# Low parts of the weight tiles on VectorE, rounding of h on ScalarE, in a two-layer streaming encoder

## The reference, cut to what matters

```python
D_MODEL, SEQ, DEPTH = 1024, 512, 2          # D_FF = 2816
for l in range(DEPTH):
    ada = (silu(c) @ w_ada[l] + b_ada[l]).reshape(B, 9, D_MODEL)
    u = modulate(rmsnorm(x, norm_g[l, 0]), ada[:, 0], ada[:, 1])
    x = x + 0.5 * ada[:, 2] * swiglu(u, w_ff1_up[l], w_ff1_down[l])
    u = modulate(rmsnorm(x, norm_g[l, 1]), ada[:, 3], ada[:, 4])
    x = x + ada[:, 5] * token_mixing(u, ...)      # window attention + causal pools, two gates, w_out
    u = modulate(rmsnorm(x, norm_g[l, 2]), ada[:, 6], ada[:, 7])
    x = x + 0.5 * ada[:, 8] * swiglu(u, w_ff2_up[l], w_ff2_down[l])
# swiglu(u): a, b = split(u @ w_up); (silu(a) * b) @ w_down
# token_mixing: z = u @ w_in; q, k, v, p, g_a, g_p = split(z)
#   merged = sigmoid(g_a) * (attention(q, k, v) @ w_attn_o) + sigmoid(g_p) * (pools(p) @ w_pool_o)
#   merged @ w_out
```

## Time and profile before

| what | value |
|---|---|
| median of 3 runs | 2163.26 us (2158.65 to 2165.34) |
| span of the profiled execution | 2167.4 us |
| TensorE busy | 2103.8 us |
| VectorE busy | 987.4 us |
| GpSimd busy | 955.2 us |
| ScalarE busy | 571.0 us |
| mean granted TensorE clock | 0.978 |

### The profile page before, as it was taken

The page is one execution under the profiler, slowest core; times in us unless marked ns, Lnnn a source line. Parts: engine busy times, 40 slices in busy tenths (PEclk is TensorE's granted clock), DMA queues, the critical chain, the costliest instruction groups (busy, mean ns, idle before and its releaser), DMA issues.

```text
span 2167.4 us, 30219 instructions
## 1 busy us (share of the span) xinstructions
PE 2103.8 (97%) x10214; PEld 1775.1 (82%) x10214; DVE 987.4 (46%) x1609; ACT 571.0 (26%) x850; POOL 955.2 (44%) x471
## 2 busy tenths in 40 slices
PE   7999999998999999999999999999989999999999
PEld 7888888886887888878888888888868788888887
DVE  5733234268658643223345422335856766332332
ACT  1322222231422422222222222222233224123222
POOL 0644344345245554334445533444443456443443
PEclk6999999999999999999999999999999999999999
DMA  7344345332345355254425524442423544432333
GB/s 272 108 136 140 91 146 163 71 117 83 93 127 183 88 162 161 68 146 137 136 59 172 155 75 145 137 134 67 141 69 112 156 151 126 131 100 79 98 100 104
DMA packets 343634, 267.49 MB, mean 123 GB/s; under 512 B 27094, under 2 KB 306990, under 8 KB 343470
## 3 DMA queue, kind: packets, MB, share of 16 engines
q1 hardware_dynamic: 341792, 264.80, 40.8%
q10 hardware_dynamic: 1678, 0.55, 0.1%
HBM read 263.21 MB, written 2.10 MB: 122 GB/s over the span
## 4 chain that ended last, share of the span: by engine, by line
PE 79%; issue 12%; POOL 5%; DVE 2%; DMA 1%; ACTq 0%; DVEq 0%; POOLq 0%; ACT 0%; SPq 0%
PE bank L1214 23%; PE bank L1215 22%; PE bank L1216 22%; POOL w_lo L561 5%; PE bank L1277 1%; PE bank L1278 1%; PE bank L1281 1%; PE ps L1485 1%; PE ps L1299 1%; POOL pool_s L575 1%; PE ps L1237 1%; PE ps L1236 1%; PE ps L1235 1%; PE bank L1235 1%; PE bank L1237 1%
## 5 line engine op out<-in xcount | busy, mean ns | idle before, releaser
L561 POOL TENSOR_TENSOR w_lo<-stage,w_hi 128x1024 fp32r<-128x1024 f32 (+2 forms) x342 | 856.8, 2519 | 1107.2 <-ACT w_hi L619 1060.2
L1214 PE MATMUL bank<-u_hi,w_hi 128*128 128x512 f32 x1792 | 713.2, 398 | 10.5 <-issue 7.5
L1215 PE MATMUL bank<-u_lo,w_hi 128*128 128x512 f32 x1792 | 701.4, 391 | 0.0
L1216 PE MATMUL bank<-u_hi,w_lo 128*128 128x512 f32 x1792 | 701.3, 391 | 0.0
L619 ACT ACTIVATE w_hi<-stage 128x1024 fp32r<-128x1024 f32 (+2 forms) x340 | 353.5, 1071 | 207.2 <-DMA stage<-in_w_pool_o 66.3
L1214 PEld LDWEIGHTS bank<-u_hi,w_hi 128*128 128x128 f32 x1792 | 339.2, 189 | 82.9 <-issue 11.8
L1216 PEld LDWEIGHTS bank<-u_hi,w_lo 128*128 128x128 f32 x1792 | 338.9, 189 | 72.0
L1215 PEld LDWEIGHTS bank<-u_lo,w_hi 128*128 128x128 f32 x1792 | 339.4, 189 | 70.9 <-issue 2.9
L1214 PE MATMUL bank<-h_hi,w_hi 128*128 128x512 f32 x744 | 292.1, 393 | 6.1 <-POOL w_lo L561 6.1
L909 DVE TENSOR_TENSOR prod<-silu,bank 128x512 f32<-128x512 f32 x88 | 60.5, 687 | 515.9 <-PE bank L1216 493.1
L889 DVE SCALAR_TENSOR_TENSOR ada_acc<-ada_stage,c_act,ada_acc 128x512 f32<-128x512 f32 x252 | 268.0, 1064 | 52.5 <-DMA ada_stage<-in_w_ada 47.9
(11 more groups left out here) (160 smaller groups left out, 1680.6 us busy)
## 6 DMA issues: line engine op xcount, KB each, us to landing
stage<-in_w_ff_up SPq DMA_DIRECT2D x176, 512.0 KB
ada_stage<-in_w_ada SPq DMA_DIRECT2D x256, 256.0 KB, 3.5
stage<-in_w_ff_down SPq DMA_DIRECT2D x32, 1408.0 KB
stage<-in_w_in SPq DMA_DIRECT2D x18, 1024.0 KB
stage<-in_w_out SPq DMA_DIRECT2D x10, 1024.0 KB
ada_first<-in_w_ada SPq DMA_DIRECT2D x16, 512.0 KB, 12.2
stage<-in_w_in SPq DMA_DIRECT2D x16, 256.0 KB
stage<-in_w_in SPq DMA_DIRECT2D x8, 512.0 KB
```

Of the source, the lines that this page charges most:

```text
L561: nc.gpsimd.tensor_tensor(stage_tile(w_lo, kind, n), t, hi_tile(n, depth(kind, n)), ALU.subtract).then_inc(lo_ready, 1)
L1214: mm(bank[n % BANKS][:, :], hi[:, k, :], rhs_hi(k), start=(k == 0), stop=False)
L1215: mm(bank[n % BANKS][:, :], hi[:, k, :], rhs_lo(k), start=False, stop=False)
L1216: last = mm(bank[n % BANKS][:, :], lo[:, k, :], rhs_hi(k), start=False, stop=(k == k_n - 1))
```

## The change

VectorE makes the low parts of the weight tiles in the layers (in the mix at the front of its step for steps 0 to 5 and 26 to 49, and behind the step's other work, ahead of the ada pieces, for steps 6 to 25; in the feed-forward stages at the front of every step). GpSimd keeps the low parts of u, the pools' sums, and the first tiles before the layers. ScalarE rounds the product to h_hi, after it has rounded the weights in the same odd step, and waits for the product for that. In an odd step VectorE does its ada piece between the product and h_lo.

```diff
--- before.py
+++ after.py
@@ -589,12 +589,8 @@
                 low_part("ff", 0, n)
             with pool.Fori(0, DEPTH) as l:
                 u_low(l, 0)
-                with pool.Fori(0, 2) as half:
-                    for n in range(FF_TILES):
-                        low_part("ff", tiles_before(l, 0, half), n + AHEAD)
                 u_low(l, 1)
                 for n in range(MIX_TILES):
-                    low_part("mix", tiles_before(l, 1), n + AHEAD)
                     if n == 1:
                         for t in (*pool_in, *pool_s):
                             nc.gpsimd.memset(t[:, 0:PAD], 0.0).then_inc(pads_zeroed, 1)
@@ -602,9 +598,6 @@
                     if T_P - 1 <= n < T_P + 3:
                         window_sums(l, n - T_P + 1)
                 u_low(l, 2)
-                with pool.Fori(0, 2) as half:
-                    for n in range(FF_TILES):
-                        low_part("ff", tiles_before(l, 2, half), n + AHEAD)
 
 
 
@@ -647,6 +640,10 @@
                             act.wait_ge(product_ready, products_before(l, i, half) + j - 1)
                         nc.scalar.activation(silu[:, j % 2, :], bank[n % BANKS][:, :], ACT.Silu
                                              ).then_inc(silu_ready, 1)
+                    if n < 2 * HALF_FT and n % 2 == 1:
+                        j = n // 2
+                        act.wait_ge(product_ready, products_before(l, i, half) + j + 1)
+                        nc.scalar.activation(h_hi[:, j, :], prod[:, j % 2, :], ACT.Copy).then_inc(h_hi_ready, 1)
                     if n >= 2 * HALF_FT:
                         square(x_before(l, i, half), n - 2 * HALF_FT, adds_before(l, i, half))
 
@@ -772,6 +769,13 @@
                     ins = nc.vector.scalar_tensor_tensor(y, t, 1.5, y, ALU.add, ALU.mult)
                 ins.then_inc(newton, 1)
 
+            def low_part(kind, base, n):
+
+                dve.wait_ge(hi_ready, base + n + 1)
+                t = stage_tile(stage, kind, n)
+                nc.vector.tensor_tensor(stage_tile(w_lo, kind, n), t, hi_tile(n, depth(kind, n)),
+                                        ALU.subtract).then_inc(lo_ready, 1)
+
             def vectors(l, i):
 
                 count = l * VEC_STEPS + 2 + i * 3
@@ -900,6 +904,7 @@
                 tiles = tiles_before(l, i, half)
                 count = products_before(l, i, half)
                 for n in range(FF_TILES):
+                    low_part("ff", tiles, n + AHEAD)
                     if n < 2 * HALF_FT and n % 2 == 1:
                         j = n // 2
                         dve.wait_ge(silu_ready, count + j + 1)
@@ -908,8 +913,8 @@
                             dve.wait_ge(h_lo_ready, count + j)
                         nc.vector.tensor_tensor(prod[:, j % 2, :], silu[:, j % 2, :], bank[n % BANKS][:, :], ALU.mult
                                                 ).then_inc(product_ready, 1)
-                        dve.wait_ge(product_ready, count + j + 1)
-                        nc.vector.tensor_copy(h_hi[:, j, :], prod[:, j % 2, :]).then_inc(h_hi_ready, 1)
+                        if n < FF_ADA:
+                            ada_piece(l, i, half, n)
                         dve.wait_ge(h_hi_ready, count + j + 1)
                         nc.vector.tensor_tensor(h_lo[:, j, :], prod[:, j % 2, :], h_hi[:, j, :], ALU.subtract
                                                 ).then_inc(h_lo_ready, 1)
@@ -919,7 +924,7 @@
                         ada_group(l, i, half, n // 8 - 1)
                     if n == 18:
                         make_gate(l, i, half)
-                    if n < FF_ADA:
+                    if n < FF_ADA and (n % 2 == 0 or n >= 2 * HALF_FT):
                         ada_piece(l, i, half, n)
 
             def read_tile(tiles, n, dst):
@@ -1053,6 +1058,8 @@
             def mix(l):
                 tiles = tiles_before(l, 1)
                 for n in range(MIX_TILES):
+                    if not T_P <= n < T_Y:
+                        low_part("mix", tiles, n + AHEAD)
 
                     if T_P + 2 <= n <= T_P + 5:
                         pool_mix(l, n - T_P - 2)
@@ -1102,6 +1109,8 @@
                         merged(l, n, tiles)
                     if n >= T_OUT:
                         update_x(l, 1, 0, n - T_OUT, n, tiles)
+                    if T_P <= n < T_Y:
+                        low_part("mix", tiles, n + AHEAD)
                     if n in MIX_SUMS and n != T_V:
                         ada_group(l, 1, 0, MIX_SUMS[n])
                     for a, step in enumerate(MIX_STEPS):
```

## The result

The changed kernel takes 2213.3 us (median of 4 runs, 2206.9 to 2216.5) where the kernel before takes 2162.8: ratio 1.0231, 95% interval 1.0208 to 1.0253, so it is slower. Its profiled execution took 2215.4 us, with a span of 2213.6 (before 2167.4) and a mean clock of 0.974. The kernel before was run again beside each group of experiments (medians 2160.4 to 2162.7 us), and the ratio given with an experiment is to those runs.

What follows compares the result with a forecast made beforehand. TensorE was taken as the bound, busy 2103.8 of 2167.4 us. Terms 40 - 9 + 4 + 11 = +46, plus 2 for half clock, gave 2163.3 + 48 = 2211 us; range 2180 to 2240, the forecast's own 2195 to 2226.

Steps and rivals of the forecast that it cites:

- the loop: Mix tiles 26 to 41: load, w_hi, low part, merge, ada piece, next load take 10.4 us per two tiles; +40 us.
- the clock behind the waits: Half clock on TensorE behind the new waits: 2 us added to the sum.
- Pools: Mix tiles 6 to 11: group_pool 3.4 to 4 us earlier, with part of the clock's loss 4.5 a layer; -9 us.
- The wait for pool_in: Sign at the pools: TensorE's wait for VectorE's pool_in, 6.02 us before, goes down to 2 to 3 us.
- Ends: Ten ends of halves and mixes: low part delays the update of x, 8 x 0.85 + 2 x 1.9; +11 us.
- waits of 0.8 to 2 us ahead of L1251: Sign that the forecast is right: TensorE waits of this length ahead of that source line.
- Tiles 0 to 5: Start of the mix: v_t's copy waits behind a low part, +3.2 us second layer, +0.4 first; +4 together.
- Feed-forward: Feed-forward stages: VectorE needs 5.4 us per two tiles against TensorE's 10.9; cost nothing but their ends.
- VectorE's busy time: Whole kernel: VectorE ends near 1214 us, 56%, with some 30 us back from other forms; no bound as a total.
- Faster: Rival: loads come in time, the loop doesn't close, waits in the earlier trace go too; 2154 us, chance 0.08.
- Much slower: Rival: each new wait at the ten ends and in the loop also drops the clock; 2235 us, chance 0.18.
- No change: Rival: loop takes half its length and ends are hidden, 20 - 9 + 2 - 11; 2165 us, chance 0.04.

Runs made afterwards that it cites:

- experiment 1: Changed kernel with the low parts of the mix's steps 26 to 49 back on GpSimd: 2162.4 us, 0.9999 of the kernel before.
- experiment 2: Changed kernel with VectorE's low part last, behind merge and ada pieces, in the mix's steps 26 to 41: 2163.0 us, 1.0003 of the kernel before.
- experiment 3: Changed kernel with VectorE's order in mix steps 26 to 41 made ada pieces, low part, merge: 2173.2 us, 1.0053 of the kernel before.
- experiment 11: Changed kernel, low part first in feed-forward steps 0 to 21 and mix 0 to 4, last in mix 5 to 41, behind x's update in the last eight: 2149.4 us.
- experiment 7: Changed kernel with the low part last in every VectorE step, feed-forward too: 2153.6 us, 0.9959 of the kernel before.
- experiment 9: Kernel before, with VectorE making only the low parts of mix steps 5 to 41, last in each step; VectorE rounds h: 2141.5 us, 0.9916.
- experiment 8: Kernel before, with VectorE making only the low parts of mix steps 5 to 11, last in each step; VectorE rounds h: 2148.7 us, 0.9933.
- experiment 6: Changed kernel, low part last in mix steps 26 to 41 and behind x's update in the last eight steps of halves and mix: 2153.8 us, 0.9967 of before.
- experiment 4: Changed kernel with the rounding of h back on VectorE, so the low parts' move alone: 2212.4 us, 1.0241 of the kernel before.
- experiment 5: Kernel before, with ScalarE rounding h and VectorE's ada piece between product and h_lo in odd steps: 2161.4 us, 0.9996.
- experiment 12: Kernel before, with VectorE making the low parts of mix steps 5 to 41, last in each step, and ScalarE rounding h: 2144.0 us, 0.9917.

## Why the prediction was right

**The direction and the size.** 2211 us were forecast and 2213 came. The largest term was the loop, and it is what the runs show: experiments 1 and 2 take it away and land on the time of before, 3 shows which link carries it (40 of 50 us the load behind the ada piece, the rest the merge).

**Term by term.** *Loop:* +40 forecast, +44.1 in the traces. The turn of 10.4 us was right; with the 5.0 us added by which the kernel after is ahead at tile 26, load 44 was forecast 1.5 us too early, the last merge 0.7 us. What the sum had left out of this term is the clock behind the waits, for which I had put 2 us in all: 0.52 for 6.4 us after the wait of 8.84 (window below) is 3 us in the first layer alone.
*Pools:* -9 forecast, -14.1 measured. Most of what was mis-sized is the clock again. The wait for pool_in fell to 1.61 us, below my 2 to 3, so group_pool came 4.4 us earlier where I had 3.4 to 4; and of the 2.4 us lost at 1.2 GHz I had counted only 0.5 to 1.1 as won, and all of it went. Timelines of the kernel after, answering to the earlier trace rows, and the windows behind that wait, behind the wait of 3.36 us in the loop and behind tile 42's, answering to the earlier trace rows:

```profile
526.68 0.69 DVE L992 TENSOR_TENSOR h_lo<-pool_y,h_hi 128x512 fp32r<-128x512 f32 x1
527.29 1.22 DVE L776 TENSOR_TENSOR w_lo<-stage,w_hi 128x1024 fp32r<-128x1024 f32 x1
528.43 0.75 DVE L893 SCALAR_TENSOR_TENSOR ada_acc<-ada_stage,c_act,ada_acc 128x512 f32<-128x512 f32 x1
...
529.88 0.17 DVE L980 TENSOR_TENSOR pool_in<-edge,pool_in 128x16 f32<-128x16 f32 x1
...
530.11 1.12 PE L1380 MATMUL ps<-pool_in,pool_w 128*128 128x512 f32 x2 [1.61 <-DVE pool_in L980]
```
```profile
530.10:535.00 4.90, 4.89 (x20) 3.73 (x21) 3.66 (x5) 0.00 (x0) 0.00 (x0) 1.00 0.60 166
...
664.80:670.70 5.90, 5.88 (x14) 4.64 (x15) 4.80 (x8) 0.00 (x0) 0.00 (x0) 0.50 0.19 52
...
705.60:712.00 6.40, 6.40 (x16) 5.01 (x17) 3.79 (x5) 0.63 (x1) 0.00 (x0) 0.52 0.76 245
```

The same two instructions of VectorE that took 2.74 and 2.82 us take 0.69 and 0.75. The rule of the Trainium skill that the prediction named beside the earlier trace rows (GPSIMD Engine Reference, § 8 Key points: contention for the shared SBUF interfaces) fits these rows; it tells where time comes back, not that TensorE gets it: VectorE's pieces have a mean of 746 ns in the changed kernel and in experiment 11, and 64 us lie between the two.
*Attention:* no term, +5.9 measured. This is what the prediction missed, and it is the same mechanism as the loop, so the walk should have gone through every stage with new waits:

```profile
551.17 1.23 DVE L776 TENSOR_TENSOR w_lo<-stage,w_hi 128x1024 fp32r<-128x1024 f32 x1 [2.87 <-ACT w_hi L612]
552.32 0.15 DVE L901 TENSOR_TENSOR ada_sum<-ada_sum,ps 128x4 f32<-128x4 f32 x1
...
552.52 1.13 PE L1391 MATMUL ps<-probs_t,v_win 128*128 128x512 f32 x2 [1.72 <-DVE ada_sum L901]
```

The small addition for an ada group is queued behind a low part that waits 2.87 us, and TensorE waits for the addition. In these steps the low part already stood behind attention's own work, but ahead of the ada work; last in the step it costs nothing (experiments 7, 9 and 11; in 8 the low parts beside attention are on GpSimd).
*Ends:* +11 forecast, 8.5 measured by the same matmuls (experiment 6): the mix's ends cost 3.7 (3.8 forecast), a half end 0.50 to 0.64 in place of 0.85. The sign that I had named for them, waits of 0.8 to 2 us ahead of L1251, came only at the two mix ends (1.0 us, for the added squares); at the halves the waits are 0.3 us. *Tiles 0 to 5:* +4, with two half ends 5.7; the table has 6.0, but also -1.8 and -4.1 for experiments 8 and 9, where only the low part of step 5 was moved there, so one execution doesn't confirm this term. *Feed-forward:* nothing, and so it is: in the middle of the halves TensorE has no wait above 0.25 us, and experiments 4, 5 and 12 show the same for the rounding of h.

So the mechanism and the largest term were right, but that the sum came out within 3 us is in part luck: two errors, -5 at the pools and +6 in attention, cancel. VectorE's busy time was put at 1214 us and is 1160: the low parts and the ada pieces were right to 1 us, but the other forms got back about 85 us (987.4 + 424.9 - 87.1 - 80 = 1245), not 30. It changed nothing, since VectorE's total is no bound.

**The rivals.** *Faster* needed the loads to come in time; they come in time when the low part stands behind the ada piece, and then the whole change is 0.6% faster (experiment 11), by the pools and the waits of the earlier trace rows as that rival said. *Much slower* didn't come, but not because the clock held: behind the wait of 3.36 us it was at 0.50 for 5.9 us (window above), longer than in the earlier trace rows. It cost no more time because the loads set the pace there: TensorE's slower matmuls only shorten its next wait, and the merge that releases tile 42's last block comes no later. Only what the clock lost behind tile 42's wait was added, 3 us in the first layer. *No change* had a slip in its sum: with the ends hidden their term is nothing, not -11, so 20 - 9 + 2 is +13, about 2176; the measured time is far from both.

## What to carry to other kernels

An instruction that waits for a load and is moved to an in-order engine holds up everything behind it; ask first what in that queue the next load waits for, because the two together close a loop whose turn holds the load's whole latency. Here the place in the queue was worth 64 us (2213.3 against 2149.4), and the choice of engine 14 at the pools and some 8 in tiles 26 to 42. Work can be split by stage: two engines that stall each other should be kept apart where the late one is what the bound engine waits for, and seven instructions a layer were enough for 14 of the 20 us that were to be had (experiments 8 and 9).

## What the runs showed of the hardware

A low part on GpSimd makes VectorE's instruction of 0.69 us with two inputs in SBUF last 2.74, about the length of GpSimd's own (8.10 for three), and such work is long in all kernels with that overlap: the ada pieces have a mean of 1064 ns before, 1145 with h rounded by ScalarE (experiment 5), 746 after. It isn't the number of inputs alone. The cast of one input was held too (1.84 us at 526.31 before, 0.43 at 537.50), and an instruction that takes one of its two inputs from PSUM was not. Two groups of the kernel before:

```profile
L914 DVE TENSOR_TENSOR h_lo<-prod,h_hi 128x512 fp32r<-128x512 f32 x88 | 82.9, 943 | 3.0
L909 DVE TENSOR_TENSOR prod<-silu,bank 128x512 f32<-128x512 f32 x88 | 60.5, 687 | 515.9 <-PE bank L1216 493.1 <-ACT silu L648 22.8
```

After, h_lo has a mean of 692 ns and the product still 687, though 80 of its 88 instructions had run beside one of GpSimd before.

I had not expected that one wait alone tells so little of the clock. After 1.61 us at the pools it stayed at 1.00 (2.4 GHz), above; after 3.36 it was at 0.50 (1.2 GHz) and after 8.84 at 0.52. In experiment 8, second mix, a wait of 0.99 us was followed by 4 us near the lower level:

```profile
1514.29 1.05 PE L1348 MATMUL ps<-consts_s,squares 128*128 128x2 f32 x8 [0.99 <-ACT squares L685]
```
```profile
1515.00:1519.00 4.00, 4.00 (x14) 3.17 (x14) 1.86 (x1) 0.81 (x2) 4.00 (x2) 0.57 0.94 292
```

What sets it was not tried. It is also why entries of 1 to 3 us of the table are not argued from.
